# Block sums of the up weights by accumulating DMAs, and down-weight high parts by GpSimd

## What is computed

```
def conv_ffn(xn, buf, w_up, w_conv, b_conv, w_down):
    u, gt = jnp.split(xn @ w_up, 2, axis=-1)
    t = u.shape[1]
    up = jnp.concatenate([buf.astype(u.dtype), u], axis=1)
    conv = b_conv
    for j in range(CONV_W):
        conv = conv + w_conv[j] * up[:, j:j + t]
    y = (jax.nn.silu(conv) * gt) @ w_down
    return y, up[:, -(CONV_W - 1):]
```

## Time and profile before

| | us |
|---|---|
| median of 3 runs | 1810.85 |
| lowest and highest | 1810.84, 1811.95 |
| the profiled execution | 1809.74 |
| its span | 1808.0 |
| TensorE busy | 1615.9 (89%) |
| VectorE busy | 1167.4 (65%) |
| ScalarE busy | 716.5 (40%) |
| GpSimd busy | 454.5 (25%) |
| GpSimd's block sums, 144 | 227.2 |

### The profile page before, as it was taken

How to read it: one execution, slowest core, us unless ns; L and a number is a source line. 1 busy time by engine, 2 the same in 40 slices (tenths; PEclk the granted TensorE clock), 3 DMA queues, 4 the chain that set the end, 5 groups by cost and what they waited for, 6 DMA issues and landing times.

```text
span 1808.0 us, 37313 instructions
## 1 busy us (share of the span) xinstructions
PE 1615.9 (89%) x14375; PEld 1445.7 (80%) x14375; DVE 1167.4 (65%) x2502; ACT 716.5 (40%) x1585; POOL 454.5 (25%) x450
## 2 busy tenths in 40 slices
PE   6999999879898889797989999998898979888897
PEld 5899865569898879797889997555898979788896
DVE  4434456665778786968563344575658796876865
ACT  3322256543244352524342213663433453343524
POOL 1001114421423242424001101352124241422321
PEclk9999999999999999999989999999999999999999
DMA  9345495585312223222133538516851222222211
GB/s 344 106 117 181 144 306 196 154 220 112 121 45 94 71 94 94 71 71 71 51 93 93 181 97 289 173 57 193 141 186 47 71 71 94 71 71 71 94 48 55
DMA packets 194001, 219.55 MB, mean 121 GB/s; under 512 B 12042, under 2 KB 153802, under 8 KB 193372
## 3 DMA queue, kind: packets, MB, share of 16 engines
q1 hardware_dynamic: 188928, 201.45, 36.5%
q0 software_dynamic: 4896, 15.71, 3.3%
HBM read 208.77 MB, written 16.68 MB: 125 GB/s over the span
## 4 chain that ended last, share of the span: by engine, by line
PE 61%; DVE 16%; DVEq 8%; ACT 7%; issue 5%; DMA 1%; SPq 1%; POOL 0%; ACTq 0%
PE ps L1652 15%; PE ps L1041 12%; PE ps L1471 6%; DVEq L3046 6%; PE ps L1531 4%; PE ps L884 3%; DVE slab_r L3071 2%; DVE big_r L2362 2%; PE ps L1180 2%; PE ps L1092 2%; PE ps L1165 2%; DVE slab_r L2362 2%; PE ps L1025 1%; ACT big L2096 1%; DVE big L3026 1%
## 5 line engine op out<-in xcount | busy, mean ns | idle before, releaser
L3345 POOL TENSOR_TENSOR slab<-slab 128x512 f32<-128x512 f32 x144 | 227.2, 1578 | 488.6 <-DMA slab<-in_w_up 195.5
L1041 PE MATMUL ps<-slab_r,work_r 128*128 128x256 f32 x960 | 205.8, 283 | 0.0
L1531 PE MATMUL ps<-work_r 128*128 128x272 f32 x576 | 154.4, 292 | 21.1 <-DVE side_r L3071 19.0
L2121 ACT ACTIVATE work_r<-slab 128x512 fp32r<-128x512 f32 x126 | 78.5, 623 | 229.3 <-PE ps L1531 227.1
L1652 PE MATMUL ps<-side_r,big_r 128*128 128x272 f32 x696 | 149.4, 297 | 21.4 <-DVE big_r L2362 21.4
L1041 PEld LDWEIGHTS ps<-slab_r,work_r 128*128 128x128 f32 x960 | 157.9, 188 | 2.6 <-issue 2.5
L1652 PE MATMUL ps<-side_r,slab_r 128*128 128x272 f32 x696 | 147.2, 294 | 0.0
L1652 PE MATMUL ps<-big_r 128*128 128x272 f32 x696 | 146.6, 293 | 0.0
L1531 PE MATMUL ps<-work_r,slab_r 128*128 128x272 f32 x552 | 128.5, 291 | 13.9 <-DVE slab_r L3071 13.9
L1652 PEld LDWEIGHTS ps<-side_r,big_r 128*128 128x128 f32 x696 | 111.9, 193 | 25.4 <-DVE big_r L2362 24.0
L1531 PEld LDWEIGHTS ps<-work_r 128*128 128x128 f32 x576 | 104.6, 190 | 25.4 <-issue 18.3
(11 more groups left out here) (550 smaller groups left out, 4651.6 us busy)
## 6 DMA issues: line engine op xcount, KB each, us to landing
slab<-in_w_mod SPq DMA_DIRECT2D x22, 2048.0 KB, 10.7
slab<-in_w_up SPq DMA_DIRECT2D x72, 512.0 KB, 5.2
slab<-in_w_in SPq DMA_DIRECT2D x20, 1024.0 KB, 5.7
slab<-in_w_down SPq DMA_DIRECT2D x20, 1024.0 KB, 6.6
slab<-in_cache_cmp_kv SPq DMA_DIRECT2D x128, 128.0 KB, 2.0
slab<-in_cache_sel_kv SPq DMA_DIRECT2D x96, 128.0 KB, 2.1
big<-in_cache_win_kv SPq DMA_DIRECT2D x16, 512.0 KB, 7.5
slab<-in_w_up SPq DMA_DIRECT2D x8, 1024.0 KB, 22.3
```

Of the source, the lines that this page charges most:

```text
L1041: ins = mm(ps[n % 4][:, 0:cw], x, fr(wt[:, k, :]), start=k == 0 and m == 0, stop=k == KC - 1 and m == 2)
L1531: ins = mm(ps[bank][:, 0:HALF], wt, fr(x[:, k, :]), start=new and k == 0 and m == 0, stop=k == 3 and m == 2, skip_group_check=True)
L2121: A_(fr(ring_hi[n % RING]), src, ACT.Copy).then_inc(b_hi.sem, 1)
L3345: G(wsum[kind], a, b, op).then_inc(b_sum.sem, 1)
```

## The change

1. **Signs.** The gate is computed negated, so that all weight sums are additions: M5 = G_K1 + G_K2, M6 = U_K1 + M5, M3 = U_K2 + M6, M7 = G_K1 + U_K1. Input sums change their signs to suit, and the gate product multiplies by -1.
2. **Sums by DMA.** SyncE loads the first terms U_K1, U_K2 and G_K1 a second time, into the three buffers of M6, M3 and M7 (`load_sums`, three DMAs of 256 KB). GpSimd then issues four DMAs per chunk that add one SBUF block to another (`block_sums`). M5 is formed in place in the raw buffer. M6 waits for M5 to have landed, M3 for M6.
3. **Down weights.** The high parts of groups 1 to 4 are made by GpSimd after the sums of chunks 4j+2 and 4j+3, no longer by ScalarE in chunks 4j+1 and 4j+2; VectorE's low parts move to chunks 4j+2 and 4j+3 too. Group 0 and the last one stay as they were.
4. Some semaphores of the attention stage share one (no work moves there).

The diff, cut to its core:

```diff
-        wsum = {kind: slab[0][:, 512 * i:512 * i + 512] for i, kind in enumerate(("M5", "M6", "M3", "M7"))}
+        sums = {kind: slab[0][:, 512 * i:512 * i + 512] for i, kind in enumerate(("M6", "M3", "M7"))}
...
+                def load_sums(c):
+
+                    def term(kind, h, k, sem):
+
+                        sp.dma_start(sums[kind].rearrange("p (k n) -> p k n", k=4),
+                                     wup[L, :, 4 * k:4 * k + 4, h, 128 * c:128 * c + 128]).then_inc(sem, 16)
+
+                    if c == CL:
+                        sp.wait_ge(g_acc.sem, g_acc.at(CL, L))
+                    else:
+                        sp.wait_ge(*low_at("M3", c - 1, L))
+                    term("M6", 0, 0, chain_in)
+                    term("M3", 0, 1, chain_in)
+                    if c > CL:
+                        sp.wait_ge(*low_at("M7", c - 1, L))
+                    term("M7", 1, 0, third_in)
...
+                for c in range(CL + 2, FC):
+                    load_sums(c)
+                    if c + 1 < FC:
+                        load_raw(c + 1)
+                    if c % 4 == 1:
+                        load_down(c // 4)
...
-                    if g < NG and q in (1, 2):
-                        if q == 1:
-                            act.wait_ge(slab_in[1], slab_loads("ffn", 1, L, g))
-                        split_down(2 * q - 2, 1)
                     product5_out(c)
                     high("M7", c)
...
-                    tt(hid[:, q, 0:HALF], gate2, cv[:, 1, 0:HALF], ALU.mult)
+                    stt(hid[:, q, 0:HALF], gate2, -1.0, cv[:, 1, 0:HALF], ALU.mult, ALU.mult)
...
                     low_block("M3", c)
-                    if g < NG and q in (1, 2):
-                        split_down(2 * q - 2, 1, g)
+                    if g < NG and q in (2, 3):
+                        split_down(2 * q - 4, 1, g)
                     low_block("M7", c)
...
+                def block_sums(c):
+
+                    def added(dst, src, kind):
+
+                        pool.dma_start(dst, src, accum_op=ALU.add).then_inc(sum_at(kind, c, L)[0], 16)
+
+                    pool.wait_ge(*raw_loads(c, L))
+                    added(up_block(c, G_K1), up_block(c, G_K2), "M5")
+                    pool.wait_ge(third_in, 16 * nth_chunk(c, L) + 16)
+                    added(sums["M7"], up_block(c, U_K1), "M7")
+                    pool.wait_ge(chain_in, 32 * nth_chunk(c, L) + 32)
+                    pool.wait_ge(*sum_at("M5", c, L))
+                    added(sums["M6"], up_block(c, G_K1), "M6")
+                    pool.wait_ge(*sum_at("M6", c, L))
+                    added(sums["M3"], sums["M6"], "M3")
...
+                for c in range(CL, FC):
+                    block_sums(c)
+                    if c // 4 < NG and c % 4 in (2, 3):
+                        if c % 4 == 2:
+                            pool.wait_ge(slab_in[1], slab_loads("ffn", 1, L, c // 4))
+                        for k in (2 * (c % 4) - 4, 2 * (c % 4) - 3):
+                            nc.gpsimd.tensor_copy(fr(hiD[:, k, :]), slab[1][:, D * k:D * k + D]).then_inc(d_hi.sem, 1)
```

More of the change, by code:

```diff
@@ L339, in trunk_program, with block_of @@
         U_K1, U_K2, G_K1, G_K2 = range(4)
-        wsum = {kind: slab[0][:, 512 * i:512 * i + 512] for i, kind in enumerate(("M5", "M6", "M3", "M7"))}
+        sums = {kind: slab[0][:, 512 * i:512 * i + 512] for i, kind in enumerate(("M6", "M3", "M7"))}
+        def block_of(kind, c):
+            if kind in sums:
+                return sums[kind]
+            return up_block(c, {"M1": U_K1, "M2": U_K2, "M4": G_K2, "M5": G_K1}[kind])
         ring_hi = [work[:, 9984:10496], big[:, 0:512], up[:, 0, 0:512], slab[0][:, 2048:2560]]
@@ L542, in trunk_program @@
                                     sig("dec_probsT_copied_dve", 2), sig("dec_pv", 4))
-        d_cmb, d_out = sig("dec_combined", 2), sig("dec_out", 1)
+        d_cmb = sig("dec_combined", 2)
+        d_sums = sig("dec_heads_stacked_decay_spread_num_out_mix_transposed", 5)
+        ms_m, ms_dec, ms_num, d_out, ms_t = [Part(d_sums, i) for i in range(5)]
         KEYS_STORED = 16 * (1 + NB + 2 + 2 + 1 + NB)
@@ L601, in high_at, with nth_chunk @@
             return b_hi.sem, b_hi.at(n + 1 + (4 if n >= 2 else 0), L)
+        chain_in, third_in = [ctx.enter_context(nc.semaphore(n)) for n in ("sums_2_4_first_terms_loaded", "sum_3_first_term_loaded")]
+        sums12, sum3, sum4 = [ctx.enter_context(nc.semaphore(n)) for n in ("sums_1_and_2_added", "sum_3_added", "sum_4_added")]
+        def nth_chunk(c, L):
+            return L * (FC - CL) + c - CL
         def sum_at(kind, c, L):
-            return b_sum.sem, b_sum.at(4 + 4 * (c - CL) + ("M5", "M6", "M3", "M7").index(kind) + 1, L)
+            n = nth_chunk(c, L)
+            return {"M5": (sums12, 32 * n + 16), "M6": (sums12, 32 * n + 32), "M3": (sum4, 16 * n + 16), "M7": (sum3, 16 * n + 16)}[kind]
         def low_at(kind, c, L):
@@ L796, in _ @@
                 load_raw(CL + 1)
+                load_sums(CL)
+                load_sums(CL + 1)
                 load_down(1)
                 load_raw(CL + 2)
-                for j in range(1, NG + 1):
-                    if j > 1:
-                        load_raw(4 * j + 2)
-                        load_down(j)
-                    for c in range(4 * j + 3, min(4 * j + 6, FC)):
-                        load_raw(c)
-                    if j == NG - 1:
-                        load_down(NG)
-                        break
+                for c in range(CL + 2, FC):
[4 more added lines that the diff above has]
+                        load_down(c // 4)
             for n, (t, hf, _) in enumerate(FINAL):
@@ L2110, in high @@
                     n = nth(kind, c)
[L2111 removed]
+                    if kind in ("M1", "M2", "M4"):
+                        act.wait_ge(*raw_loads(c, L))
+                    else:
                         act.wait_ge(*sum_at(kind, c, L))
[L2113 to L2116 removed]
                     if n >= RING:
@@ L2181, in _ @@
                 act.wait_ge(t_sum.sem, t_sum.at(4, L))
-                for _, t_, th in TSUM:
-                    A_(fr(th), t_, ACT.Copy).then_inc(t_hi.sem, 1)
+                for kind, t_, th in TSUM:
+                    A_(fr(th), t_, ACT.Copy, scale=-1.0 if kind == "M6" else 1.0).then_inc(t_hi.sem, 1)
                 high("M5", CL)
@@ L3147, in _ @@
                         low_block("M1", c + 1)
-                    if g < NG and q in (1, 2):
-                        split_down(2 * q - 1, 1, g)
+                    if g < NG and q in (2, 3):
+                        split_down(2 * q - 3, 1, g)
                     low_block("M4", c)
@@ L3327, in input_sums @@
                     pool.drain()
[L3328 removed]
+                    G(T2, T2, T1, ALU.add).then_inc(t_sum.sem, 1)
                     pool.drain()
[L3330 to L3345 removed]
@@ L3347, in _ @@
-                input_sums()
-                block_sum("M5", CL)
-                block_sum("M6", CL)
-                block_sum("M3", CL)
-                block_sum("M7", CL)
-                for c in range(CL + 1, FC):
-                    block_sum("M5", c)
-                    block_sum("M6", c)
-                    block_sum("M3", c)
-                    block_sum("M7", c)
+                    G(T4, T2, T4, ALU.subtract).then_inc(t_sum.sem, 1)
+                def block_sums(c):
[10 more added lines that the diff above has]
+                    added(sums["M3"], sums["M6"], "M3")
```

56 lines of the change are left out of this document (19 added, 37 removed).

## The result

The changed kernel takes 1907.8 us (median of 4 runs, 1906.6 to 1911.3) against 1811.4 for the kernel before beside it: a ratio of 1.0535, with a 95% interval of 1.0517 to 1.0553. The forecast was 1785 and its range ended at 1838, so both the sign and the range are wrong. The profiled execution took 1907.6 us.

A forecast was written before the change was run, and what follows sets the result against it. VectorE, slowed by GpSimd sums, was taken to bound the stretches between down blocks. Per layer -6.6-2.4-4.1 = -13.1 us, -26 for two, gave 1810.9-26 = 1785 us, with a range from 1742 to 1838.

The forecast's parts named there:

- The bound before and the slowed VectorE: Stretches between down blocks: VectorE is the bound, slowed by GpSimd sums; three groups of its instructions lose 76 us.
- The first chunk after a down block: Product 7's low part there ends 9.4 us after the down block, in place of 13.5.
- The loop as the path: Chunk to chunk, loads and two serial accumulates set the time; a stretch takes 32.7 us plus six accumulates.
- The casts: GpSimd's down-weight copies, 1.3 us each, cost VectorE at most some 5 us per stretch, hidden under the loop.
- A, the accumulate: Landing time of one accumulating DMA in the sum loop: 3.5 us taken, 2.7 to 4.6 kept.
- The middle accumulate meets the raw load of the next chunk on the DMA engines; I add 0.3 us each: Loop of chunks 2, 3 and 0 of a group: 0.3 us added for each, 0.9 per stretch.
- the prediction's own first step: Loads in the chunk loop: 1 MB raw is 3.8 us of data; 768 KB take 4.8 from product 3's low part.
- Small terms of the loop: Chunk loop besides accumulates: loads 4.8 us, third sum's issue 0.7, wake-ups 0.1, ScalarE copy 0.62, low part 0.69.
- The 4.1 us before the last down block's chunk: End of each layer's stage: 4.1 us less before the last down block's chunk.
- The second, slower: Rival: accumulates in the sum loop take over 4.05 us; 1837 us at 4.6, 1856 at 5.0; chance 0.32.
- its last reason, the raw load: Slower rival's reason in the sum loop: the raw load's 512-byte pieces stand ahead of the accumulate.

The follow-up runs named there:

- no_sums: Kernel before with the four GpSimd block sums left out, M5, M6, M3 and M7 each taking a raw block instead; 1707.7 us.
- sums_only: Changed kernel with the down weights' high parts back on ScalarE, and VectorE's low parts with them; 1911.1 us, ratio 1.0533.
- raw_eighth: Changed kernel with raw loads from chunk 6 on bringing one eighth of their bytes, 128 KB in place of 1 MB per chunk; 1844.65 us.
- raw_later: Changed kernel with the raw load of chunk c+1 issued only when M6's accumulate of chunk c has landed; 1934.3 us.
- hybrid2: Changed kernel with down weights on ScalarE, M5 and M7 summed by DMA (M7 in two buffers), M6 and M3 by GpSimd additions; 1738.5 us, ratio 0.9604.
- casts_only: Kernel before with the high parts of down weights in groups 1 to 4 made by GpSimd, VectorE's low parts moved along; 1835.1 us, ratio 1.0131.

## Why the prediction was wrong, point by point

**The bound before and the slowed VectorE: right.** no_sums takes the additions away and frees 11 us per stretch, and in the changed kernel the subtractions take 0.68 us again except beside casts.

**The first chunk after a down block: right.** Low M7 ends 9.7 us after the block in the six stretches behind a layer's first; the step had 9.4 in place of 13.5. In the first stretches it is 18.4 and 18.1 us, where 12.5 was forecast: SyncE issues the 2 MB of the down load at 547.11, 0.2 us behind M6's accumulate, and this one takes 9.7 us (10.1 in layer 1).

**The loop as the path: right.** GpSimd waits twice in a row. ScalarE's copies wait 224 us for accumulates, and longer in all (236 us) only for TensorE, across the down blocks. TensorE waits before products 6 and 3.

**The casts: nearly hidden, as the step had them.** sums_only has the same time, though 0.4 us of VectorE's slowing shows in the loops with casts. GpSimd's busy time falls by 71 us only and not by 190, since its 144 issues count as 130 us busy; without them it is 201 less.

**A, the accumulate: right.** 3.5 us was taken, 3.3 is measured for one with nothing ahead of it. The term that the range was built on was the one that held.

**"The middle accumulate meets the raw load of the next chunk on the DMA engines; I add 0.3 us each": this is the step that failed.** The 0.3 has no working beside it; the only measure of the engines' load that the prediction names is a mean share of busy time. But the two do not meet by chance. Low M3 and low M7 release the first terms, and these let the accumulates start 5.4 us behind low M3. Low M4, 5.1 us behind low M3 in two loops of three and 3.1 or 3.8 in the third, releases the raw load. So in every loop but one the raw load, 3.8 us of data by the prediction's own first step, is issued ahead of the pair of accumulates, and in all 24 ahead of M6's. That costs M6's accumulate 2.8 us on average (7.5 against 4.6 in raw_eighth), 3.5 in the loop shown, and raw_eighth shows that it makes 73 us of the whole.

**Small terms of the loop.** The accumulates start 5.4 us behind low M3 and not 4.8. The prediction let all three loads run from low M3. The two that do have landed 4.0 us behind it; M7's is issued behind low M7, 0.8 or 1.7 us later, and lands at 5.1, and the queue's order makes M6 wait for it. M6's accumulate has M7's ahead of it and lands in 4.3 at best, 4.6 on average, even where hardly any raw load is near (raw_later, raw_eighth), not 3.5. The wake-up and the low part's end are 0.3 more, and M7's issue and M3's accumulate 0.4 less. 475.1-435.8 = 39.3 us of raw_eighth's stretches are above forecast; 33.6 of them are in the 24 loops, 1.4 us each, and the rest in the first chunks.

**The 4.1 us before the last down block's chunk: wrong.** There was no such gain. The kernel before has made its last sums by 854.4, ahead of the last long block (to 877.4), and VectorE's subtractions behind it already take 0.69 us; nothing was slowed there. I had carried a pattern of the other chunks to the end without a row. That is 8.2 us.

**TensorE's clock: not in the sum.** In the stretches the granted clock is 0.83 to 0.87, and the down blocks are 7.1 us longer. TensorE's windows after a wait (length, then busy us of PE; the clock is the third number from the end):

```profile
673.00:675.00 2.00, 1.79 (x8) 1.82 (x9) 1.83 (x6) 2.00 (x5) 0.32 (x1) 0.50 0.63 111
675.00:677.00 2.00, 2.00 (x11) 2.00 (x11) 2.00 (x4) 1.14 (x3) 0.00 (x0) 0.50 0.65 156
677.00:679.00 2.00, 2.00 (x14) 2.00 (x14) 2.00 (x5) 0.59 (x2) 0.00 (x0) 0.79 0.83 239
679.00:681.00 2.00, 2.00 (x18) 2.00 (x17) 1.88 (x5) 1.04 (x3) 0.82 (x2) 1.00 0.13 32
```

After the wait of 4.6 us that ended at 673.2 it works at 0.50, the lower of its two levels (1.2 GHz), with 11 matmuls in 2 us, and from 677.8 on at the full one with 18. Inside a stretch I take it to cost nothing more, since TensorE, busy for 50 of 66 us, waits for the next sum anyway; no run separates it. A down block that starts so takes 26.3 us in place of 24.3.

The account of the miss, from the forecast's growth of -26 to +98: 73 for the raw load's bytes, 39 for the other terms of the loop, 8 for the gain that wasn't there, 7 for the down blocks, less 3 for the earlier start. That makes 124.6 for a miss of 124.1 in the profiled executions.

**The rivals.** The second, slower, had the sign and the waits, at 1837 or 1856; its price for A was not what happened, and only its last reason, the raw load, was. The collision had a half-sentence in it, and should have been a timeline: the order of VectorE's program has low M4 some 5 us behind low M3, the one releases the raw load and the other the first terms, and laying the two side by side would have shown them meet.

## What to carry to other kernels

When a change makes a loop out of transfers, write down for each one what else is issued within a few microseconds ahead of it, by following both releases back to the instructions that cause them; a mean share of busy DMA engines says nothing of two streams released by the same engine. Order the issues of a queue by who needs the result first, since each also waits for what the ones ahead of it wait for: that alone was worth 60 us here. And move only that work to the DMAs which can be started a whole turn ahead with a second buffer, as hybrid2 does; in series an addition of 1.3 to 1.6 us on GpSimd beats an accumulate of 3.3 or more.

## What was not expected of the hardware

- An accumulating DMA of 256 KB within SBUF lands 3.3 us after its issue with nothing ahead of it, 4.3 with another one issued 0.53 us before, and 5.4 to 9.0 (mean 7.5) with a 1 MB load ahead too. Its issue is 0.86 us in GpSimd's records, and a second one starts 0.53 us after the first. That is no dearer than a plain load of the size (3.3 us in the DMA issues above), though it reads two operands.
- A 1 MB load of another queue ahead adds 2.8 us on average to the second of two such DMAs, and in pieces of 4096 bytes little less than in pieces of 512. The first packet of the pair moves 3.3 us after the issue, 1.4 with nothing ahead.
- Two casts of 128x1024 to fp32r take GpSimd 2.3 us in the changed kernel, while VectorE's subtraction beside them takes 3.02 in place of 0.68. In casts_only they take 2.9 to 3.5, with subtractions of 1.5 us beside them.
- TensorE at half its clock after a wait of 4.6 us, for 4.6 us.
